# SwiGLU in hidden groups of 8, 8 and 6 tiles, and the mixing's opening weights one by one behind the last four down tiles

## What is computed

```python
D_FF = ((8 * D_MODEL // 3 + 127) // 128) * 128      # 2816 = 22 tiles of 128

def swiglu(x, wg, wu, wd):
    hid = jax.nn.silu(jnp.einsum('btd,df->btf', x, wg)) * jnp.einsum('btd,df->btf', x, wu)
    return jnp.einsum('btf,fd->btd', hid, wd)

def hybrid_layer(x, ...):
    x = layer_norm(ALPHA * x + 0.5 * swiglu(x, ffn1_wg, ffn1_wu, ffn1_wd), ln1_g, ln1_b)
    z = jnp.einsum('btd,de->bte', x, w_in)
    c_g, b_g, h, p, g_a, g_p = jnp.split(z, SPLITS, axis=-1)
    ...
    x = layer_norm(ALPHA * x + jnp.einsum('btd,de->bte', m, w_out), ln2_g, ln2_b)
    x = layer_norm(ALPHA * x + 0.5 * swiglu(x, ffn2_wg, ffn2_wu, ffn2_wd), ln3_g, ln3_b)
```

## Time and profile before

| | us |
|---|---|
| median of 3 runs | 1044.84 (1044.74 to 1045.28) |
| the profiled execution | 1046.54 |
| its span | 1044.7 |
| TensorE busy | 1031.5 (99% of the span) |
| VectorE (DVE) busy | 711.8 (68%) |
| ScalarE (ACT) busy | 482.5 (46%) |
| GpSimd (POOL) busy | 460.4 (44%) |
| HBM traffic | 102 MB, 98 GB/s over the span |

### The profile page before, as it was taken

One profiled execution on the slowest core, in us unless ns is written; L12 is line 12 of the kernel. 1 busy time (PEld: TensorE's weight loads), 2 busy tenths in 40 slices (PEclk: granted clock), 3 DMA queues, 4 the chain that ended last, 5 costly groups with the idle time before them and its releaser, 6 DMA issues.

```text
span 1044.7 us, 21275 instructions
## 1 busy us (share of the span) xinstructions
PE 1031.5 (99%) x8592; PEld 1026.5 (98%) x8592; DVE 711.8 (68%) x1144; ACT 482.5 (46%) x735; POOL 460.4 (44%) x358
## 2 busy tenths in 40 slices
PE   8999999999999999999999999999999999999997
PEld 7999999999999999999999999999999999999997
DVE  6987977898755845822524325789888788977276
ACT  3665535645554452332332324456653565456335
POOL 4333444344348354844553546332425433443530
PEclk9999999999999999999999999999999999999999
DMA  8133343334327210532342334203333332432502
GB/s 256 52 102 102 102 121 87 103 97 122 112 83 195 82 40 13 156 103 85 87 117 67 113 89 127 67 14 102 91 112 102 102 116 77 132 101 82 144 20 82
DMA packets 195829, 103.32 MB, mean 99 GB/s; under 512 B 5188, under 2 KB 194260, under 8 KB 195725
## 3 DMA queue, kind: packets, MB, share of 16 engines
q1 hardware_dynamic: 195651, 101.86, 33.9%
q10 hardware_dynamic: 82, 0.12, 0.1%
HBM read 99.74 MB, written 2.48 MB: 98 GB/s over the span
## 4 chain that ended last, share of the span: by engine, by line
PE 93%; DVE 3%; issue 1%; DMA 1%; ACT 0%; SPq 0%; POOL 0%; DVEq 0%; ACTq 0%; POOLq 0%
PE ps L1641 19%; PE ps L1642 19%; PE ps L1643 19%; PE ps L1664 10%; PE ps L1661 10%; PE ps L1662 10%; PE ps L1710 2%; PE ps L1717 1%; PE ps L1711 1%; PE ps L1785 1%; DMA xrow<-in_x_prompt_dram 1%; PE ps L1764 1%; PE ps L2123 0%; DVE xl L1087 0%; DMA raw<-in_ffn_wg_dram 0%
## 5 line engine op out<-in xcount | busy, mean ns | idle before, releaser
L672 POOL TENSOR_TENSOR wl<-raw,wh 128x512 fp32r<-128x512 f32 (+1 forms) x168 | 223.9, 1362 | 328.7 <-DVE raw L1147 313.0
L719 ACT ACTIVATE wh<-raw 128x1024 fp32r<-128x1024 f32 (+4 forms) x183 | 210.4, 1154 | 175.0 <-DMA raw<-in_ffn_wg_dram 57.8
L1642 PE MATMUL ps<-form_lo,wh 128*128 128x260 f32 x640 | 181.5, 284 | 0.0
L1643 PE MATMUL ps<-form_hi,wl 128*128 128x260 f32 x640 | 181.3, 283 | 0.0
L1641 PE MATMUL ps<-form_hi,wh 128*128 128x260 f32 x640 | 181.3, 283 | 0.0
L1661 PE MATMUL ps<-xh,wh 128*128 128x260 f32 x640 | 166.9, 282 | 0.0
L1662 PE MATMUL ps<-xl,wh 128*128 128x260 f32 x640 | 166.5, 282 | 0.0
L1641 PE MATMUL ps<-xh,wh 128*128 128x260 f32 x536 | 152.1, 284 | 2.8 <-POOL wl L672 2.1
L1642 PE MATMUL ps<-xl,wh 128*128 128x260 f32 x536 | 151.8, 283 | 0.0
L1643 PE MATMUL ps<-xh,wl 128*128 128x260 f32 x536 | 151.5, 283 | 0.0
L659 POOL TENSOR_TENSOR wl<-raw,wh 128x512 fp32r<-128x512 f32 x63 | 88.0, 1396 | 138.9 <-ACT wh L719 138.8
(11 more groups left out here) (288 smaller groups left out, 2478.5 us busy)
## 6 DMA issues: line engine op xcount, KB each, us to landing
raw<-in_ffn_wg_dram SPq DMA_DIRECT2D x80, 256.0 KB, 3.3
raw<-in_w_in_dram SPq DMA_DIRECT2D x40, 512.0 KB, 4.0
b<-in_ffn_wu_dram SPq DMA_DIRECT2D x40, 256.0 KB, 3.4
raw<-in_ffn_wu_dram SPq DMA_DIRECT2D x40, 256.0 KB, 3.0
raw<-in_ffn_wd_dram SPq DMA_DIRECT2D x16, 512.0 KB, 5.5
raw<-in_ffn_wd_dram SPq DMA_DIRECT2D x24, 256.0 KB, 3.5
raw<-in_ffn_wd_dram SPq DMA_DIRECT2D x24, 192.0 KB, 2.9
raw<-in_w_out_dram SPq DMA_DIRECT2D x7, 512.0 KB, 3.8
```

The lines of the kernel that those rows point to most:

```text
L672: nc.gpsimd.tensor_tensor(slots(wl_slot, s, p), slots(raw_slot, s, p), slots(wh_slot, s, p).bitcast(F32), ALU.subtract).then_inc(lo_ready, 1)
L719: return nc.scalar.activation(out, in_, ACT.Copy)
L1642: mm(out, hi, vl, start=False, stop=False, skip_group_check=more)
L1643: ins = mm(out, lo, vh, start=False, stop=n == count, skip_group_check=more)
```

## The change

The last group shrinks from 8 to 6 hidden tiles and the middle one grows from 6 to 8, in both SwiGLUs. In the first SwiGLU the four opening chunks of the mixing move: each is loaded, rounded and split behind one of down 4, 5, 6 and 7. The diff (the load and placement loops follow the same rule as the split shown here):

```diff
-    GROUPS = (8, 6, 8)
+    GROUPS = (8, 8, 6)
...
                     load((n, "down", d), column(wd_v[n], d)[:, GROUP_AT[-1]:KF, :])
-                    if (n, d) == (0, 3):
-                        load(("mix", 0), column(win_v, P_AT))
-                        load(("mix", 1), column(win_v, C_AT))
-                    elif (n, d) == (0, 4):
-                        load(("mix", 2), column(win_v, H_AT))
-                    elif (n, d) == (0, 5):
-                        load(("mix", 3), column(win_v, B_AT))
+                    if n == 0 and d >= 4:
+                        load(("mix", d - 4), column(win_v, (P_AT, C_AT, H_AT, B_AT)[d - 4]))
...
                     split((n, "down", d))
-                    if n == 0 and d in (3, 4, 5):
-                        for j in {3: (0, 1), 4: (2,), 5: (3,)}[d]:
-                            split(("mix", j))
+                    if n == 0 and d >= 4:
+                        split(("mix", d - 4))
...
                 round_chunk((n, "down", 3))
+                round_chunk((n, "down", 4))
                 if n == 0:
                     round_chunk(("mix", 0))
-                    round_chunk(("mix", 1))
-                round_chunk((n, "down", 4))
-                if n == 0:
-                    round_chunk(("mix", 2))
                 square_tile(2 * n, 0)
                 round_chunk((n, "down", 5))
                 if n == 0:
-                    round_chunk(("mix", 3))
+                    round_chunk(("mix", 1))
                 square_tile(2 * n, 1)
                 square_tile(2 * n, 2)
                 round_chunk((n, "down", 6))
+                if n == 0:
+                    round_chunk(("mix", 2))
                 square_tile(2 * n, 3)
                 round_chunk((n, "down", 7))
+                if n == 0:
+                    round_chunk(("mix", 3))
```

More of the change, by code:

```diff
@@ L456, in build @@
                 chunk_place((n, "down", d), DOWN_AT[d], 2)
-                if n == 0 and d in (3, 4, 5):
-                    for j in {3: (0, 1), 4: (2,), 5: (3,)}[d]:
-                        open_place(("mix", j), j, MIXED, number[0, "P7", NU])
+                if n == 0 and d >= 4:
+                    open_place(("mix", d - 4), d - 4, MIXED, number[0, "P7", NU])
             if n == 0:
```

## The result

The changed kernel takes 1059.08 us in the median of four runs (1058.10 to 1061.29), the kernel before 1044.79 beside it: ratio 1.0132, 95% interval 1.0115 to 1.0149, slower by 14 us. 1058.3 was forecast, in a range of 1050.8 to 1063.0.

A forecast was written before the change was run, and what follows sets the result against it. TensorE was taken as the bound, busy 1031.5 of 1044.7 us. Matmuls -2.9, waits +9.2 and +5.1, clock +2.1 gave +13.5 us: 1060.0 for the profiled execution, median 1058.3 us, range 1050.8 to 1063.0.

The forecast's parts named there:

- the matmuls (-2.9 us): Whole kernel: 12 fewer matmuls per SwiGLU, 24 in all at 0.12 us each; larger middle-group pieces charged nothing.
- The mechanism: SwiGLU ends: TensorE waits for POOL's splits of down 6 and 7, and at four stat_sums for DVE's sums.
- Waits of the first SwiGLU (9.2 us): End of first SwiGLU: 0.2 at down 5, 2.0 at down 6, 4.3 at down 7, 1.3 and 1.4 at stat_sums.
- the one on holds behind down 6: First SwiGLU: four POOL operations (4.45 us) and DVE sums between them (some 2.1) make down 7 ready at 345.5.
- the lower bound: First SwiGLU: if POOL never held TensorE, DVE alone would still make it wait 5.2 us.
- Waits of the second SwiGLU (5.1 us): End of second SwiGLU: 1.2 at down 6, 0.9 at down 7, 0.7 and 2.1 at stat_sums, 0.2 at transposes.
- The clock (2.1 us): First SwiGLU's 4.3 us gap: 0.4 uncovered; one more halving behind short gaps at the sums: 1.7; bounds 0.4 and 6.
- Only the long gap costs clock: Rival, 22%: waits as forecast, no halving behind the short gaps; 1056.6 us.
- Everything stays covered: Rival, 4%: down 6 and 7 split in time, DVE's sums before TensorE; only -2.9, so 1042.0 us.
- Only DVE's chain holds: Rival, 20%: POOL and ACT get through, waits 5.2 + 4.8, clock little; 1052.4 us.
- The clock falls after most gaps: Rival, 12%: three more halvings that nothing covers, 5.1 us; 1063 us.
- The rounding of down 6: First SwiGLU: ACT's rounding should start within a microsecond of 336 less the place shift of +10.1 us.

The follow-up runs named there:

- The groups alone: Kernel before with its groups of 8, 6, 8 tiles made 8, 8, 6, the mixing's chunks left in place: 1060.1 us, ratio 1.0138.
- the early splits: Changed kernel with down 6 rounded and split right behind down 5, down 7 behind the second square: 1060.7 us, ratio 1.0138 to the kernel before.
- The idle matmuls: Changed kernel with matmuls on a free PSUM bank filling TensorE's waits in both SwiGLUs and the middle norm: 1053.4 us, ratio 1.0067 to the kernel before.
- its own fill: Kernel before with eight idle matmuls in TensorE's 0.90 us gap ahead of the middle norm's first stat_sums: 1044.8 us, ratio 0.9991.
- the order alone: Kernel before, groups still 8, 6, 8, with only the new order of the chunks: ratio 1.0023, 2.4 us slower.

## Why the prediction was right, and where it was not

**What bounds the kernel, and the matmuls (-2.9 us).** Right in number: the page has 24 fewer, and the larger units of the middle group brought no wait. The prediction misread the waits of the kernel before, though. The three longest are not 2.1, 0.9 and 0.7 us: there are others of 2.0, 1.7, 1.7 and 1.5 us, and the last of these is at the end of a SwiGLU, at the last transposes. No term of the sum rests on it.

**The mechanism.** Right in most places: waits at down 6's and down 7's splits and at the second `stat_sums` of both SwiGLUs. Four waits at `stat_sums` were forecast; the two first ones show no named wait. The groups alone and the early splits show that the shorter cover brings the loss with any of the three orders tried. What it is too short for is not a fixed length. DVE's chain without its waits for TensorE was 23.7 and 22.3 us before and is 25.3 and 21.2 now, for the 19.9 that TensorE leaves, and 6.6 and 2.3 us of it are holds by POOL. Less the holds it would be some 18.6 and 18.9 us, under the 19.9 (an estimate from the rows). By this the cover runs short only together with the holds. No run here takes POOL's splits away from DVE's sums, so what that would give is not shown.

**Waits of the first SwiGLU (9.2 us).** Over-sized. Between DVE's first add and the first `stat_sums`, 5.76 us of matmuls left and 0.5 us was gained (6.6 to 6.1), so 5.3 us were waited against the 7.8 of the text; to the second, 2.9 left and 1.8 was gained, 1.1 against 1.4. The step that failed is the one on holds behind down 6. Down 6's split was ready 15.4 us after DVE's start, against 15.75 forecast (339.0 less 323.25). Down 7's was ready after 20.9, against 22.25, and the last sum after 25.3, against 27.55. The hand-overs between DVE and POOL fell better than in my lay-out: POOL's four operations behind down 6's split took 5.4 us with their holds, not 6.5. The truth lies between my lay-out and the lower bound, and nearer the bound: 6.4 us of waits, against 9.2 and 5.2. The first `stat_sums` was hardly waited for.

**Waits of the second SwiGLU (5.1 us).** Also over-sized at first: 14.7 to 10.4 is 4.2 of 5.76, so 1.5 us were waited, against 2.8; the splits of down 6 and 7 are named with 0.9 and 0.2 us of it. Behind it 9.3 to 10.4 is 1.1 of 2.88: 1.8 us, and 0.6 at the transposes, against 2.3. The 3.9 us in all lie below what I had called the least, 4.8. That bound took DVE's present 25.3 us less 2.9 of idle time, 22.4, as fixed; beside the narrower splits it was 21.2, with holds of 2.3 us for 3.2. The waits of both ends together are 5.3 + 1.1 + 1.5 + 1.8 + 0.6 = 10.3 us, against 14.3.

**The clock (2.1 us).** Under-sized, and in the wrong places: 3.2 us in the middle norm and some 3.0 in the tail, against a full and a partly covered halving in the first SwiGLU. Of the 3.6 us behind the last `stat_sums`, 0.6 is the wait at the transposes. I had named no cost to a stage that the change leaves alone. That the 4.3 us gap "will halve it" was wrong in its length, 3.0 us, and nothing fell behind it in two of the three traces with that gap unfilled. The rival *Only the long gap costs clock* (1056.6) falls too, and with it the rule that the prediction takes from the Trainium skill (TensorE: Matmul & The Clock Gate, Part 1: The HAM clock gate), read strictly: the falls that cost most came behind a 0.99 us gap followed by one-column sums and, in the tail, behind waits of 1.4 and 0.6 us. The idle matmuls put the clock's whole cost in the filled places at 6.8 us; the kernel before pays 0.9 of it too, as its own fill shows. Against that kernel the term is then about 6, at my upper bound. The prediction called itself wrong if the clock were halved for much more than two stretches of some 3.5 us. It was halved for some 10 and 16 us, so by its own sign this part was wrong.

**The sum.** -2.9 + 10.3 + 6.2 - 0.7 = +12.9, the span. The -0.7 comes from the opening: in the execution of before the clock had fallen at 50 us, for 1.7 us; in that of the change it had not, but a wait of 0.9 us came at 53 us. The forecast +13.5 has two errors that nearly cancel: 4.0 us too much waiting and about 4 too little clock. That they cancel is luck: the number was right for partly wrong reasons.

**The other rivals.** *Everything stays covered* is refuted. *Only DVE's chain holds* has the sum of the waits nearly right, 10.0 against 10.3, and the early splits show that the chain alone costs as much. Its mechanism is refuted, for POOL's splits did hold TensorE, by 1.6 and 3.0 us in the first SwiGLU, and it gave the clock next to nothing. *The clock falls after most gaps* (1063) is nearest on the clock, with too much waiting. **The rounding of down 6** was said to start near 336 "less the place shift of +10.1"; the shift has to be added, and 346.1 compares with 344.80.

**Left open.** What decides whether the clock falls behind a gap, and for how long. Behind the middle norm it was 3.4 us in the kernel before, some 10 in the changed kernel, and nothing in the trace of the order alone, whose gap is as long (0.93 us). Behind the 3.0 us gap at down 7 it fell in one execution and not in two others. The places vary between executions, and no run here separates them.

## What to carry to other kernels

When TensorE never waits, the slack of what feeds it is invisible in the waits; before moving matmuls away from a stage, add up the chain of the other engines there and compare it with the matmuls that will be left (here 23.7 us of DVE between two marks, for 19.9 of TensorE). Take out the time in which that chain itself waits for TensorE, and count the holds apart, for they change with what stands beside them. Moving the feeding work about inside such a stage only moved the wait here. Price a gap on TensorE at its length and again for the clock behind it, and look for that second price in stages that the change does not touch.

## What the runs showed of the hardware

- Idle matmuls made a kernel faster: six fills, none of them useful work, took 6.8 us off 1059 (give or take 2.4).
- A gap's length did not tell whether the clock falls. 3.0 us of standing still between full matmuls left it at 2.4 GHz in two traces, while in a third, with the same gap, it was at 1.2 GHz behind it (0.50 at 354 us). 0.99 us followed by 16 one-column matmuls was followed by 10 us at 1.2 GHz, and 0.93 us with the same matmuls behind it (the order alone) by none. A gap of 4.6 us (early splits) had 0.68 and then 0.50 in windows of 4 us from 356 us on.
- A DVE sum of two SBUF operands one column wide took 1.19 us beside a POOL split and 0.16 us without one; it ended with the split under way.
